# Ending differential attention: head sums in column tiles, their reciprocal on 128 partitions, spreads in one-pass float32r, and three waits moved in the Fourier stage

## What is computed

```python
def fourier_mix(f):                                    # layer 0, 4 groups of 128 channels
    z = f.reshape(b, l, FOURIER_GROUPS, FOURIER_DIM)
    y = jnp.fft.fft2(z, axes=(1, 3), norm='ortho').real
...
def diff_attn_core(q, k, v, lam):                      # layer 1
    s = jnp.einsum('bhiqd,bhikd->bhiqk', q, k) * (q.shape[-1] ** -0.5)
    p = jax.nn.softmax(s, axis=-1)
    a = p[:, :, 0] - lam * p[:, :, 1]
    return jnp.einsum('bhqk,bhkd->bhqd', a, v)
...
def head_out(o):                                       # o: (b, 512 tokens, 8 heads, 128)
    o = rms_norm(o, subln_g, SUBLN_EPS) * (1.0 - lam_init)
    return o.reshape(o.shape[0], o.shape[1], DIFF_V_WIDTH) @ w_out
```

## Time and profile before

| | us |
|---|---|
| runs | 1644.17, 1646.96, 1646.53 (median 1646.53) |
| the profiled execution | 1643.41 |
| its span from first to last instruction | 1641.6 |
| TensorE busy in it | 1614.4 (98%) |
| VectorE, ScalarE, GpSimd busy | 977.3, 518.7, 620.1 |

### The profile page before, as it was taken

One profiled execution on the slowest core, in us unless ns is written; L12 is line 12 of the kernel. 1 busy time (PEld: TensorE's weight loads), 2 busy tenths in 40 slices (PEclk: granted clock), 3 DMA queues, 4 the chain that ended last, 5 costly groups with the idle time before them and its releaser, 6 DMA issues.

```text
span 1641.6 us, 23975 instructions
## 1 busy us (share of the span) xinstructions
PE 1614.4 (98%) x9331; PEld 1434.8 (87%) x9331; DVE 977.3 (60%) x1295; ACT 518.7 (32%) x925; POOL 620.1 (38%) x404
## 2 busy tenths in 40 slices
PE   8999999999999999999999999999999999999997
PEld 5889888989999999999999888878858988888887
DVE  4696137338865755864784678139954734435264
ACT  4422356325211211211121511248843522222222
POOL 2421376226323332422331534254503644444441
PEclk9999999999999999999999999999999999999998
DMA  9483312213153234233332122100101323222221
GB/s 360 173 296 115 109 46 76 98 40 130 65 183 99 77 98 148 101 99 118 103 111 95 65 90 90 65 14 1 41 0 65 105 101 103 90 100 92 96 84 52
DMA packets 50638, 163.98 MB, mean 100 GB/s; under 512 B 6505, under 2 KB 8809, under 8 KB 46961
## 3 DMA queue, kind: packets, MB, share of 16 engines
q1 hardware_dynamic: 50544, 162.68, 28.7%
HBM read 159.77 MB, written 2.10 MB: 99 GB/s over the span
## 4 chain that ended last, share of the span: by engine, by line
PE 92%; DVE 3%; issue 1%; DMA 1%; ACT 1%; SPq 0%; POOL 0%; POOLq 0%; DVEq 0%; ACTq 0%
PE ps L1632 26%; PE ps L1633 26%; PE ps L1634 26%; PE ps L2138 2%; PE ps L2100 2%; PE ps L2127 1%; PE ps L2005 1%; PE ps L1993 1%; PE ps L2033 1%; PE ps L1837 1%; DMA mod_big<-w_mod_dram 1%; DVE h L1257 1%; DMA raw<-units_dram 1%; PE ps L2028 1%; DVE tmp_a L1248 1%
## 5 line engine op out<-in xcount | busy, mean ns | idle before, releaser
L591 POOL TENSOR_TENSOR w_lo<-raw,w_hi 128x1024 fp32r<-128x1024 f32 (+1 forms) x237 | 485.9, 2062 | 862.6 <-ACT w_hi L750 862.4
L1632 PE MATMUL ps<-h,w_hi 128*128 128x384 f32 (+2 forms) x1176 | 409.7, 348 | 1.7 <-DVE h L1257 1.3
L1633 PE MATMUL ps<-h,w_lo 128*128 128x384 f32 (+2 forms) x1176 | 407.6, 347 | 0.0
L1634 PE MATMUL ps<-h,w_hi 128*128 128x384 f32 (+2 forms) x1176 | 407.2, 346 | 0.0
L750 ACT ACTIVATE w_hi<-raw 128x1024 fp32r<-128x1024 f32 x189 | 199.8, 1057 | 390.8 <-PE ps L1634 384.7
L1632 PE MATMUL ps<-hid_lo,w_hi 128*128 128x384 f32 (+2 forms) x800 | 277.6, 347 | 0.0
L1633 PE MATMUL ps<-hid_hi,w_lo 128*128 128x384 f32 (+2 forms) x800 | 276.5, 346 | 0.0
L1634 PE MATMUL ps<-hid_hi,w_hi 128*128 128x384 f32 (+2 forms) x800 | 276.4, 346 | 0.0
L1632 PEld LDWEIGHTS ps<-h,w_hi 128*128 128x128 f32 x1176 | 221.3, 188 | 25.2 <-issue 2.5
L1634 PEld LDWEIGHTS ps<-h,w_hi 128*128 128x128 f32 x1176 | 221.2, 188 | 16.3
L1633 PEld LDWEIGHTS ps<-h,w_lo 128*128 128x128 f32 x1176 | 221.3, 188 | 16.1
(11 more groups left out here) (224 smaller groups left out, 2259.7 us busy)
## 6 DMA issues: line engine op xcount, KB each, us to landing
raw<-units_dram SPq DMA_DIRECT2D x189, 512.0 KB, 3.3
mod_ring<-w_mod_dram SPq DMA_DIRECT2D x96, 256.0 KB, 3.3
mod_big<-w_mod_dram SPq DMA_DIRECT2D x16, 1024.0 KB, 10.5
mod_late<-w_mod_dram SPq DMA_DIRECT2D x8, 1024.0 KB, 7.6
xl<-x_dram SPq DMA_DIRECT2D x2, 2048.0 KB, 8.2
bias<-bias_dram SPq DMA_DIRECT2D x8, 384.0 KB, 3.6
xc<-ctx_dram SPq DMA_DIRECT2D x2, 1024.0 KB, 10.3
out_dram<-out_t SPq DMA_DIRECT2D x16, 128.0 KB, 1.9
```

The lines of the kernel that those rows point to most:

```text
L591: ins = nc.gpsimd.tensor_tensor(w_lo[:, s, sl], raw[:, s, sl], w_hi[:, s, sl].bitcast(F32), op=ALU.subtract)
L1632: mm(out, a[0], b[1], start=start, stop=False)
L1633: mm(out, a[1], b[0], start=False, stop=False)
L1634: return mm(out, a[0], b[0], start=False, stop=stop)
```

## The change

- `sub_sums` now puts the four blocks of 128 tokens on four 32-column tiles of the array: the stationary operand has 32 columns, the moving one 128 tokens, the output is partitions 32q to 32q + 31 by 128 columns. Epsilon terms likewise (`l_wide`, 32 columns; the last head broadcast). Unused columns are filled with ones.
- The root and the reciprocal therefore work on 128x128 (`head_root`, `head_scales`). DVE also splits the reciprocal into `sub_rh` and `sub_rl`, both float32r; the last head's is made at h == 5 of DVE's loop (before: at h == 3).
- `spread_head` takes, for each block q, one column of a float32r identity (`pick`), broadcast to 128 columns, as the stationary operand: 8 one-pass matmuls of 128 columns instead of 2 passes of 512.
- Order on PE: heads 0 to 3 are summed ahead of `turn1(30, 1)`, heads 4 to 6 right behind it, both ahead of the last `weigh1` of tiles 28 and 29; heads 0 and 1 are spread around `turn1(31, 1)`, ahead of the last two `weigh1`; the last head is summed inside the unit pair, at k == 1.
- ACT loads the root's table by a root of a constant right behind `turned1(30, 0)`. DVE makes `pick` and the ones of `l_wide` in iteration 29.
- The table `selh` and its DMA go; `oneh` grows from 64 to 224 columns.
- Layer 0: `early_mm(4)` moves from behind unit 4 to behind unit 5. The first Fourier step waits for `qk_out` 7, the third for 8; `mod_done` is awaited at step 4, and by ACT ahead of its first `u_hi`. Table unit 0 waits per group g for `u_lo` 7 + g (the copy that frees its bank), table unit 4 for all 12.

```diff
-        sub_r = at("sub_r", [P, 2, LAT], F32, x_at + size(KT, LAT))
+        oneh = at("oneh", [P, HEADS - 1, 32], F32, k1_at + size(TOK) + size(LAT))
+        sub_r = at("sub_r", [P, 2, 2, P], F32, x_at + size(KT, LAT))
+        sub_rh = at("sub_rh", [P, 2, P], F32R, x_at + size(KT, LAT) + size(4, P))
+        sub_rl = at("sub_rl", [P, 2, P], F32R, x_at + size(KT, LAT) + size(6, P))
+        l_wide = at("l_wide", [P, 4, 32], F32, k1_at + size(6, TOK) + size(LAT))
+        pick = at("pick", [P, P], F32R, k1_at + size(6, TOK) + size(LAT) + size(4, 32))
...
+            def head_root(g):
+                act.wait_ge(sub_mm, g + 1)
+                nc.scalar.activation(sub_r[:, 0, g], ps[:, g, 0:P], ACT.Sqrt, scale=1.0 / P).then_inc(sub_sqrt, 1)
+
+            def head_high(h):
+                act.wait_ge(sub_t, h + 1)
+                nc.scalar.activation(o1_hi[:, h], sub_x[:, h % 2], ACT.Copy, scale=subg[:, 1:2]).then_inc(sub_hi, 1)
...
+            turned1(N1 - 2, 0)
+            nc.scalar.activation(stat[:, 63:64], eps_c[:, 0:1], ACT.Sqrt)
+            turned1(N1 - 2, 1)
+            head_root(0)
+            out_copy(N1 // 2 - 2)
+            turned1(N1 - 1, 0)
+            turned1(N1 - 1, 1)
+            head_high(0)
+            head_high(1)
+            out_copy(N1 // 2 - 1)
             act.wait_ge(sub_sq, HEADS - 1)
             act.wait_ge(o1, HEADS * PAIRS)
             nc.scalar.activation(osq[HEADS - 1][:], o_raw[:, HEADS - 1], ACT.Square).then_inc(sub_sq, 1)
-            act.wait_ge(sub_mm, 2)
-            nc.scalar.activation(sub_last[:, 0], ps[0:1, 1], ACT.Sqrt, scale=1.0 / P).then_inc(sub_sqrt, 1)
-            for h in range(HEADS):
-                act.wait_ge(sub_t, h + 1)
-                nc.scalar.activation(o1_hi[:, h], sub_x[:, h % 2], ACT.Copy, scale=subg[:, 1:2]).then_inc(sub_hi, 1)
+            head_high(2)
+            head_high(3)
+            head_root(1)
+            for h in range(4, HEADS):
+                head_high(h)
...
+                    st.wait(V.tensor_copy(pick[:], ident[:]))
+                    st.wait(V.memset(l_wide[:, :, HEADS - 1:], 1.0))
+                    eps_terms(l_wide[:, :, 0:HEADS - 1].rearrange("p t h -> p h t"), 0, N1 - 4)
...
+            def head_scales(g):
+                dve.wait_ge(sub_sqrt, g + 1)
+                st.wait(V.reciprocal(sub_r[:, 1, g], sub_r[:, 0, g]))
+                st.wait(V.tensor_copy(sub_rh[:, g], sub_r[:, 1, g]))
+                tt(sub_rl[:, g], sub_r[:, 1, g], sub_rh[:, g].bitcast(F32), op=ALU.subtract).then_inc(sub_rec, 1)
+
+            head_scales(0)
             for h in range(HEADS + 1):
-                if h == 3:
-                    dve.wait_ge(sub_sqrt, 2)
-                    V.reciprocal(sub_last[:, 1], sub_last[:, 0]).then_inc(sub_rec, 1)
+                if h == 5:
+                    head_scales(1)
...
-                if i == 4:
+                if i == 5:
                     pe.wait_ge(f_out, 4)
-                if i in (4, 6, 8, 10):
+                if i in (5, 6, 8, 10):
                     early_mm(2 + i // 2)
...
-            pe.wait_ge(qk_out, 8)
-            pe.wait_ge(mod_done, PE_MODS)
             for n in range(2 * NT):
                 tok = slice(P * (n // 2), P * (n // 2) + P)
+                if n in (0, 2):
+                    pe.wait_ge(qk_out, 8 if n else 7)
+                if n == 4:
+                    pe.wait_ge(mod_done, PE_MODS)
...
-            pe.wait_ge(u_lo_s, 2 * NT)
             for i in range(4):
...
+                    if i == 0:
+                        pe.wait_ge(u_lo_s, 7 + g)
...
+            pe.wait_ge(u_lo_s, 2 * NT)
             for g in range(4):
...
-                last = h == HEADS - 1
+                g = h // (HEADS - 1)
                 pe.wait_ge(sub_sq, h + 1)
-                if last:
-                    mm(ps[0:1, 1], ones[:, 0:1], osq[h][:], start=True, stop=False)
-                else:
-                    mm(ps[0:HEADS - 1, 0], oneh[:, h, 0:HEADS - 1], osq[h][:], start=h == 0, stop=False)
+                for q in range(4):
+                    w = ones[:, 0:32] if g else oneh[:, h]
+                    mm(ps[32 * q:32 * q + 32, g, 0:P], w, osq[h][:, P * q:P * q + P], start=h in (0, HEADS - 1), stop=False)
                 if h >= HEADS - 2:
-                    pe.wait_ge(leps_ok, 2 if last else 1)
-                    le = l_eps[:].rearrange("p (h t) -> p t h", t=4)
-                    for t_ in range(4):
-                        tok = slice(P * t_, P * t_ + P)
-                        if last:
-                            ins = mm(ps[0:1, 1, tok], le[:, t_, h:], ident[:], start=False, stop=t_ == 3)
-                        else:
-                            ins = mm(ps[0:HEADS - 1, 0, tok], le[:, t_, 0:HEADS - 1], ident[:], start=False, stop=t_ == 3)
+                    pe.wait_ge(leps_ok, g + 1)
+                    for q in range(4):
+                        w = l_eps[:, N1 - 4 + q:N1 - 3 + q].broadcast_to([P, 32]) if g else l_wide[:, q]
+                        ins = mm(ps[32 * q:32 * q + 32, g, 0:P], w, ident[:], start=False, stop=True)
                     ins.then_inc(sub_mm, 1)
...
-            for n in range(N1 + 1):
+            for n in range(N1):
                 if n + 2 < N1:
                     scores1(n + 2)
+                if n == N1 - 1:
+                    pe.wait_ge(oneh_in, 16)
+                    for h in range(4):
+                        sub_sums(h)
                 if n >= 1:
                     turn1(n - 1, 1)
+                if n == N1 - 1:
+                    for h in range(4, HEADS - 1):
+                        sub_sums(h)
                 if n >= 3:
                     weigh1((n - 3) // 2, (n - 3) % 2)
-                if n == N1 - 1:
-                    pe.wait_ge(oneh_in, 32)
-                    for h in range(4):
-                        sub_sums(h)
-                if n == N1:
-                    for h in range(4, HEADS - 1):
-                        sub_sums(h)
-                if n < N1:
+                if n < N1 - 1:
                     turn1(n, 0)
+            weigh1(N1 // 2 - 2, 1)
+            turn1(N1 - 1, 0)
+
+            def spread_head(h):
+
+                if h >= 2:
+                    pe.wait_ge(sub_t, h - 1)
+                g, c = divmod(h, HEADS - 1)
+                pe.wait_ge(sub_rec, g + 1)
+                for q in range(4):
+                    w = pick[:, 32 * q + c:32 * q + c + 1].broadcast_to([P, P])
+                    mm(ps[:, 4 + h % 2, P * q:P * q + P], w, sub_rl[:, g], start=True, stop=False)
+                    ins = mm(ps[:, 4 + h % 2, P * q:P * q + P], w, sub_rh[:, g], start=False, stop=True)
+                ins.then_inc(sub_bc, 1)
+
+            def head_wait(k):
+
+                if k + 2 < HEADS:
+                    spread_head(k + 2)
+                if k == 1:
+                    sub_sums(HEADS - 1)
+                pe.wait_ge(sub_lo, k + 1)
+
+            spread_head(0)
+            turn1(N1 - 1, 1)
+            spread_head(1)
             weigh1(N1 // 2 - 1, 0)
             weigh1(N1 // 2 - 1, 1)
```

51 lines of the change are left out of this document (16 added, 35 removed).

## The result

The changed kernel takes 1626.5 us (median of 4 executions, 1626.17 to 1628.6), the kernel before beside it 1645.45; the ratio is 0.988, interval 0.986 to 0.990. The forecast had said faster by 14.3 us, 1632.2 with a range from 1628.0 to 1638; the measured time lies outside, 1.5 us under the lower end. The profiled executions, 1643.41 us before and 1626.17 after, differ by 17.2.

The account below looks back on a forecast made before the run. PE, busy for 98% of the span, was taken as the bound. Gains of 11.0 us at the end of attention, 2.75 in the Fourier stage and .55 at early_mm(4) made 14.3, giving 1632.2 us off the median; range 1628 to 1638.

Parts of the forecast that it names:

- item 10: End of attention: four steps of 6 product matmuls and a spread, 2.63 us each, become 2.60; .1 us gained.
- the last step: Whole kernel: the 14.3 us gain, which gives 1629.1 from the profiled execution, taken off the median instead: 1632.2 us.
- Items 1 to 4: End of attention, sums of heads 0 to 6, transposes and waits around them: .8, 2.55, .75 and 2.55 us gained.
- Items 5 and 6: End of attention: wait for last output copy and square filled, 1.3 us; last head's sum 1.83 becomes .55, 1.3 us.
- Items 7 and 8: End of attention: three spreads and a wait, .35 us gained; three product matmuls and a spread, .25 us.
- Item 9: End of attention: nine product matmuls at half clock, 3.62 us, run at full clock in 2.25; 1.4 us gained.
- the four tiles fill the array: Reason given against the rival that the clock falls again at the end of attention (1633.6 us, chance .20).
- The .3 set aside for `sub_lo`: End of attention: .3 us taken off the gain for waits on `sub_lo` at the last two heads.
- Fourier: Fourier stage: PE's waits before the first step (1.3 us) and the table unit (1.5) go; 2.75 us gained in all.
- early_mm(4): Layer 0: PE's 2.28 us wait goes, but most returns as a wait at `early_mm(5)`; .55 us gained.
- Prices: Unit costs assumed: 128-column float32r matmul .11 us, 512-column float32 pass .43, four column tiles as one, reciprocal .85.
- spreads at .081: Rival, end of attention: each spread matmul takes .081 us instead of .11, 1.9 us less, 1630.3; chance .04.

Follow-up runs that it names:

- e8_last_ahead: Changed kernel with the last head's sum put back right behind the last `weigh1`, ahead of the projection; median 1627.4 us.
- e5_rows128: Kernel before with the spreads' operands on all 128 rows (zero-padded) instead of 7, still float32 with 512 columns; median 1642.0 us.
- e12_wide_sums: Kernel before with the sums of heads 0 to 6 on 128 columns instead of 7, spreads left on 7 rows; median 1647.4 us.
- e11_rows32: Changed kernel with each spread matmul on rows 0 to 31 alone instead of all 128; median 1629.1 us.
- e6_spread_twice: Changed kernel with every spread issued twice, 64 more float32r matmuls of 128 columns; median 1633.0 us.
- e7_tiles_serial: Changed kernel with the four quarters of each sum in one column tile, one behind the other, instead of four tiles; median 1632.4 us.
- e10_merged: Changed kernel with the scales' high and low parts on different rows of one operand, so a spread is 4 matmuls instead of 8; median 1623.0 us.
- e1_early: Kernel before with only `early_mm(4)` moved one unit later; median 1645.6 us.
- e2_fourier: Kernel before with only the Fourier waits of the change; median 1644.1 us.
- e9_fill: Kernel before with five unread float32r matmuls of 512 columns in the pause ahead of the last head's sum; median 1646.0 us.

## Why the prediction was wrong

The direction, the three places and most terms held. Two steps failed: item 10 of the sum, which had almost no gain for the four steps, and the last step, which took the sum off the median. Point by point:

- *Items 1 to 4* (6.65): 6.65 in the traces. Sums and epsilon terms took 1.01 twice for .97, and the transposes a little less than counted, because a spread follows two of them after .25 and .27.
- *Items 5 and 6* (2.6): right. e8_last_ahead shows the wait of 1.2, and the last sum took .58 for .55.
- *Items 7 and 8* (.6): spreads measured .93, .92 and 1.02, not 1.03 each, and the product and spread 1.68, not 1.92: .46 more than forecast. Another .36 comes at `weigh1` and was in no item: the last 12 passes took 2.46 where item 5 had counted 2.73, the 12 before 2.69 where 2.78 stood.
- *Item 9* (1.4) at the profiled length of the fall was right: 2.17 for 2.25. That the fall would not come again was right as well (neither trace of the changed kernel has it), but "the four tiles fill the array" was not the reason: e5_rows128 ends it by the rows of the spreads alone, and e12_wide_sums keeps it with wide sums.
- *Item 10* (.1) **is the term of the sum that failed.** It carried the kernel before's gaps over ("a matmul behind a semaphore wait pays some .1 more for its weight load"). The trace after has the same semaphores at these places and no such gaps; e11_rows32 brings them back by rows alone, and e5_rows128 takes them out of the kernel before with all its waits in place. So they belong to the change between operands on few rows and on all. The .1 is paid where PE really stands still (.33 behind 1221.55, where it does), not at a semaphore that is already met. Four steps of 2.28 are 1.3 us better than four of 2.60. The .3 set aside for `sub_lo` cost .2.
- *Fourier* (2.75): 3.1, kept to the end. The waits were 1.34 and 1.57 as read; the rest is the gap behind the first matmul after each wait (.19 and .34 where .12 and .23 are the pace), which goes with the wait.
- *early_mm(4)* (.55): .4. The size was nearly right, the mechanism was not: PE waits in `half_mm` for the DMA of its weights and not before `early_mm(5)`. That both limits end within .1 us of each other was luck.
- *Prices*: .11 for a float32r matmul of 128 columns stands (.112 by e6_spread_twice). The Trainium skill, "TensorE: Matmul & The Clock Gate", section "Back-to-back issue gap", with its 81 ns, doesn't describe this stream. Column tiles at no extra cost stand by e7_tiles_serial. The reciprocal on 128 partitions, .85 forecast, took .95.

Together the sum was 2.9 us short of the difference of the two profiled executions: 2.3 at the end of attention, .35 in the Fourier stage, the .5 at PE's last two matmuls that is chance, less .2 early.

The other 2.8 us of the miss come from **the last step, "the same gain off the median gives 1632.2"**. The profiled execution of before, 3.1 us under the median, was taken as an offset that the changed kernel would keep. It didn't: the changed kernel's profiled execution is only .3 under its median. The trace of before holds the shortest fall of those seen (3.4 us), the very fall that item 9 took away, and executions of before that took 1646 to 1647 have mean clocks of .993 to .994 where it has .995. By an estimate from these figures the median execution was some 3 to 7 us longer at half clock, which is 2 to 3 us of time. Where its clock fell wasn't traced: a longer fall at the end of attention, the one near 86 us, or both. A gain priced on the shortest fall and taken off a median with more of it leaves the rest in. Without that step the forecast would have been 1629.1, still 2.6 above the measured time.

Of the rivals, none came true. The nearest in time, spreads at .081 (1630.3), is 3.8 off, and its reason is refuted by the .112 of e6_spread_twice.

Beside the page "TensorE: Matmul & The Clock Gate" of the Trainium skill: its section "Step-by-step: what each phase is for" says that a load is pulled ahead of running matmuls when the row groups don't conflict or when it goes to the background weight buffer, and that a load's time scales with its columns while the row count doesn't matter. For the load by itself the traces agree: 184 ns on 7 or 32 rows, 188 to 190 on 128. Pulled ahead it is here from all rows to all rows (gaps of 0 to .06), but between 7 or 32 rows and 128 it isn't, and that costs .3 to .4 a step.

Open: why the fall lasts 3.4 us in one execution and 13.7 in another; whether the few rows themselves or the gaps that they make bring it, since e5_rows128 removes both at once; whether 32 rows can bring it (one execution at .994 says perhaps); how often the clock falls near 86 us. Row tiles used all at once weren't tried.

## What to carry to other kernels

Look at the rows of every small stationary operand that stands between full ones: padding it with zeros to 128 rows cost no pass, took .4 us of gaps out of each step, and ended a fall of the clock. Where a profiled execution lies below the median, ask what the other executions have that it hasn't, and whether the change removes it, before carrying the difference over. Where small matmuls pace at the price of a load (.11 at 128 columns), use more rows of the operand, as e10_merged did, rather than a cheaper type. And when a wait is removed, look for every later wait that may take the lead back: here it was a DMA ten us ahead of the one that had been reckoned with.

## What was not expected of the hardware

- Gaps follow rows, not type, size or semaphores: steps of 2.24 on 128 rows and 2.63 on 7 (float32, 512 columns), 2.28 on 128 and 2.59 on 32 (float32r, 128 columns).
- The granted clock fell to 1.2 GHz during or just behind spreads on 7 rows, in all five traces of kernels that have them (before, e1_early, e2_fourier, e9_fill, e12_wide_sums), for 3.4, 6.8 or 13.7 us, and stayed down while PE was busy (12.5 of 12.5 us). Filling the pause ahead of them didn't keep it up; filling their rows did.
- A weight load starts .22 us ahead of its matmul from all rows to all rows, and together with it from all rows to 32 or 7 and back.
- The clock also fell behind a wait of 2.0 to 2.3 us between matmuls on all rows, in two of six traces, and cost 1.6 to 1.8 us.
- At 128 columns a float32r matmul costs what one pass of float32 does (steps of 2.28 and 2.27 with eight of either), while at 512 columns they stand at .23 and .43.
